# Two norms of a fused transformer block turned before their scale is known, with the scale spread as a row and multiplied in by VectorE

## The reference

```
y = x * rsqrt(mean(x * x) + 1e-6) * g              # layers
h2 = rms_norm(x, g_norm2) * (1 + sc2) + sh2        # first block, ahead of its feed-forward
u = rms_norm(h, mix_norm); proj = u @ w_in         # layers, ahead of the convolutions
dt, b, a = 48 small columns of proj                # gates of the two scans
```

## Time and profile before

| what | us |
|---|---|
| median of three runs (2225.5 to 2227.37) | 2226.86 |
| the profiled execution: its own time | 2223.37 |
| the profiled execution: its span | 2221.6 |
| PE busy | 2124.4 |
| DVE busy | 1329.9 |
| ACT busy | 1146.6 |
| POOL busy | 82.8 |

### The profile page before, as it was taken

The page is one execution under the profiler, slowest core; times in us unless marked ns, Lnnn a source line. Parts: engine busy times, 40 slices in busy tenths (PEclk is TensorE's granted clock), DMA queues, the critical chain, the costliest instruction groups (busy, mean ns, idle before and its releaser), DMA issues. The chain is left out here.

```text
span 2221.6 us, 40709 instructions
## 1 busy us (share of the span) xinstructions
PE 2124.4 (96%) x15572; PEld 1860.2 (84%) x15572; DVE 1329.9 (60%) x1821; ACT 1146.6 (52%) x1697; POOL 82.8 (4%) x90
## 2 busy tenths in 40 slices
PE   5999889999999999989999999999999998999998
PEld 4787778887888998888998887887998897998887
DVE  3436375556555996565656555555897565756554
ACT  3453644445445567654445445444557664535444
POOL 0000000000000010100000000000002010000000
PEclk9999999999999999999999999999999999999999
DMA  9663235554553544421455554555354431345553
GB/s 400 241 245 114 77 140 190 189 186 173 185 185 141 183 170 143 170 96 58 152 183 187 188 188 172 189 189 185 137 190 152 155 112 55 137 181 180 189 189 123
DMA packets 53325, 373.16 MB, mean 168 GB/s; under 512 B 6305, under 2 KB 6305, under 8 KB 9281
## 3 DMA queue, kind: packets, MB, share of 16 engines
q1 hardware_dynamic: 47664, 342.00, 42.0%
q0 software_dynamic: 5520, 29.23, 3.8%
HBM read 370.10 MB, written 1.11 MB: 167 GB/s over the span
## 5 line engine op out<-in xcount | busy, mean ns | idle before, releaser
L1470 ACT ACTIVATE HI<-ring 128x1024 fp32r<-128x1024 f32 x606 | 625.1, 1054 | 741.0 <-PE banks L549 399.2
L2020 DVE TENSOR_TENSOR LO<-ring,HI 128x1024 fp32r<-128x1024 f32 x318 | 389.1, 1226 | 369.8 <-ACT HI L1470 369.6
L2026 DVE TENSOR_TENSOR LO<-ring,HI 128x2048 fp32r<-128x2048 f32 x137 | 314.2, 2294 | 241.9 <-ACT HI L1470 241.9
L513 PE MATMUL banks<-UH,HI 128*128 128x256 f32 x1424 | 416.0, 292 | 2.7 <-DVE LO L2026 2.7
L514 PE MATMUL banks<-UL,HI 128*128 128x256 f32 x1424 | 404.0, 284 | 0.0
L515 PE MATMUL banks<-UH,LO 128*128 128x256 f32 x1424 | 403.7, 284 | 0.0
L547 PE MATMUL banks<-HI,UH 128*128 128x512 f32 x896 | 350.1, 391 | 7.1 <-DVE LO L2026 4.9
L548 PE MATMUL banks<-LO,UH 128*128 128x512 f32 x896 | 349.4, 390 | 0.0
L549 PE MATMUL banks<-HI,UL 128*128 128x512 f32 x896 | 349.2, 390 | 0.0
L513 PEld LDWEIGHTS banks<-UH,HI 128*128 128x128 f32 x1424 | 274.0, 192 | 20.5 <-issue 19.3
L514 PEld LDWEIGHTS banks<-UL,HI 128*128 128x128 f32 x1424 | 274.3, 193 | 1.9 <-issue 1.7
(11 more groups left out here) (329 smaller groups left out, 3058.1 us busy)
## 6 DMA issues: line engine op xcount, KB each, us to landing
ring<-in_w_stream SPq DMA_DIRECT2D x315, 1024.0 KB, 4.8
ARENA<-in_ada_stream POOLq DMA_DIRECT2D x16, 1024.0 KB, 5.1
ARENA<-in_ada_stream SPq DMA_DIRECT2D x8, 1024.0 KB, 15.1
GRMS<-cum_rows POOLq DMA_DIRECT2D x16, 256.0 KB, 3.6
ARENA<-in_na_bias POOLq DMA_DIRECT2D x2, 1024.0 KB, 15.2
RMS<-cum_rows POOLq DMA_DIRECT2D x8, 256.0 KB, 3.7
RSTD<-cum_rows POOLq DMA_DIRECT2D x8, 256.0 KB, 3.5
ARENA<-in_ropes POOLq DMA_DIRECT2D x1, 1088.0 KB, 20.7
```

Of the source, the lines that this page charges most:

```text
L513: nc.tensor.matmul(out, lh, rh, start=start, stop=False, **kw)
L1470: nc.scalar.activation(HI[:, q % PARTS, at], ring[:, q % RING, at], ACT.Copy).then_inc(hi_ready, 1)
L2020: nc.vector.tensor_tensor(LO[:, q % PARTS, at], ring[:, q % RING, at], HI[:, q % PARTS, at].bitcast(F32), ALU.subtract).then_inc(lo_ready, 1)
L2026: nc.vector.tensor_tensor(LO[:, q % PARTS, :], ring[:, q % RING, :], HI[:, q % PARTS, :].bitcast(F32), ALU.subtract).then_inc(lo_ready, 2)
```

## The change

Norms 1, 3 and 6 no longer build diagonals. PE transposes H unscaled (`raw_turns`) as soon as its pieces are in. When the reciprocal root is there, PE spreads it into PSUM bank 3 with two float32 products (a column broadcast against the identity), so that each partition holds the 256 tokens' scales in a row. DVE copies this row to SBUF, and makes U with one instruction a tile: turned rows times gain times scale row. In norm 1 the shift no longer goes into U: ACT adds it while it writes UH, tile by tile, and DVE while it writes UL. In the layers the small products are spread over panel 0: two tiles of k of them stand ahead of the products of each pair. The loop over panels 0 to 11 is written out, and panel 6 takes the plain order of products.

```diff
             def scaled_turns(d, banks):
-                pe.wait_ge(diag_ready, d + 1)
+                pe.wait_ge(scale_ready, d + 1)
...
+            def spread_scale(n):
+                pe.wait_ge(nrstd_ready, n + 1)
+                for t in range(2):
+                    mm = spread_tokens(bank[3][:, t * P:(t + 1) * P], NRSTD[:, t:t + 1])
+                mm.then_inc(scale_ready, 1)
+
+            def raw_turns(n, banks):
+                for p in range(KT // 2):
+                    turn_rows(n, p, banks[p])
+                spread_scale(n)
...
-            def both_tiles(outs, src, fill):
+            def both_tiles(outs, src, fill, beside=None):
...
+                    if beside is not None:
+                        beside(pair)
                     pe.wait_ge(uh_ready, KT * fill + 2 * pair + 2)
...
-            scaled_turns(1, TURN_BANKS)
+            raw_turns(1, TURN_BANKS)
...
-                scaled_turns(2 + l, TURN_BANKS)
+                raw_turns(3 + 3 * l, TURN_BANKS)
                 pe.wait_ge(pack2_loaded, 16 * l + 16)
-                for k in range(KT):
-                    pe.wait_ge(u_ready, KT * (2 + l) + k + 1)
-                    for t in range(2):
-                        mm = nc.tensor.matmul(bank[7][:, t * SMALL:(t + 1) * SMALL], ...)
-                mm.then_inc(small_done, 1)
-                with pe.Fori(0, (L_CONV - SCAN_CONV) // ROUND - 1) as r:
-                    for s in range(ROUND):
-                        wide(w0 + r * ROUND + s, ..., fill + 1 if s == 0 else None)
+                def small_products(pair):
+                    for k in (2 * pair, 2 * pair + 1):
+                        pe.wait_ge(u_ready, KT * (2 + l) + k + 1)
+                        for t in range(2):
+                            mm = nc.tensor.matmul(bank[7][:, t * SMALL:(t + 1) * SMALL], ...)
+                    if pair == KT // 2 - 1:
+                        mm.then_inc(small_done, 1)
...
+                conv_panel(0, fill + 1, small_products)
+                for j in range(1, L_CONV - SCAN_CONV - ROUND):
+                    conv_panel(j)
...
-                fill_high(u_ready, lambda k: KT * d + 2 * k + 2)
+                if shift is None:
+                    fill_high(u_ready, lambda k: KT * d + 2 * k + 2)
+                    return
+                for k in range(KT):
+                    act.wait_ge(u_ready, KT * d + k + 1)
+                    nc.scalar.activation(UH[:, k, :], U[:, k, :], ACT.Identity, bias=shift[:, k:k + 1]).then_inc(uh_ready, 1)
...
+            def raw_fill(n, d, fill, gain, shift=None, banks=TURN_BANKS):
+                dve.wait_ge(scale_ready, d + 1)
+                need(step(nc.vector.tensor_copy(RSTD[:, 0:S], bank[3][:, 0:S])))
+                def low(p):
+                    if shift is None:
+                        fill_low(fill, p)
+                        return
+                    for k in (2 * p, 2 * p + 1):
+                        dve.wait_ge(uh_ready, KT * fill + k + 1)
+                        nc.vector.scalar_tensor_tensor(UL[:, k, :], U[:, k, :], shift[:, k:k + 1], UH[:, k, :].bitcast(F32),
+                                                       ALU.add, ALU.subtract).then_inc(ul_ready, 1)
+                for p in range(KT // 2):
+                    dve.wait_ge(turned_done, 4 * n + p + 1)
+                    for e in range(2):
+                        k = 2 * p + e
+                        nc.vector.scalar_tensor_tensor(U[:, k, :], bank[banks[p]][:, e * S:(e + 1) * S], gain[:, k:k + 1],
+                                                       RSTD[:, 0:S], ALU.mult, ALU.mult).then_inc(u_ready, 1)
+                    if p:
+                        low(p - 1)
+                low(KT // 2 - 1)
...
-            diagonals(1)
-            scaled_fill(1, FILL_B1_NORM2, GS[:, 8:16], shift2)
+            raw_fill(1, 1, FILL_B1_NORM2, GS[:, 8:16], shift2)
...
-                diagonals(3 + 3 * l)
-                scaled_fill(3 + 3 * l, fill + 1, pk2("mix", 0, 8))
+                raw_fill(3 + 3 * l, 2 + l, fill + 1, pk2("mix", 0, 8))
```

More of the change, by code:

```diff
@@ L303, in build_program @@
             sem("residual_ready"), sem("squares_ready"), sem("sumsq_ready"))
-        rms_ready, nrstd_ready, diag_ready, turned_done, u_ready = (
-            sem("rms_ready"), sem("nrstd_ready"), sem("diag_ready"), sem("turned_done"), sem("u_ready"))
+        rms_ready, nrstd_ready, scale_ready, turned_done, u_ready = (
+            sem("rms_ready"), sem("nrstd_ready"), sem("scale_ready"), sem("turned_done"), sem("u_ready"))
         wide_free = sem("wide_free")
@@ L572, in both_tiles, with wide @@
                 return mm
-            def wide(w, q, rounds, par, fill=None):
+            def wide(w, q, rounds, par, fill=None, beside=None):
                 if fill is not None:
@@ L578, in wide @@
                     pe.wait_ge(wide_free, w + 1)
-                    both_tiles((bank[4 + par],), src, fill).then_inc(panel_used, 2)
+                    both_tiles((bank[4 + par],), src, fill, beside).then_inc(panel_used, 2)
                     return
@@ L987, in _, with conv_panel @@
                 ffn(1 + 2 * l, Q_LAYERS + LQ_FFN1, rounds, fill, turns(2 + 3 * l, TURN_BANKS))
-                scaled_turns(2 + l, TURN_BANKS)
+                raw_turns(3 + 3 * l, TURN_BANKS)
                 pe.wait_ge(pack2_loaded, 16 * l + 16)
-                for k in range(KT):
-                    pe.wait_ge(u_ready, KT * (2 + l) + k + 1)
-                    for t in range(2):
-                        mm = nc.tensor.matmul(bank[7][:, t * SMALL:(t + 1) * SMALL], U[:, k, t * P:(t + 1) * P],
-                                              pk2("small_w", k * SMALL, SMALL), start=(k + t == 0), stop=(k == KT - 1),
-                                              skip_group_check=True)
-                mm.then_inc(small_done, 1)
-                with pe.Fori(0, (L_CONV - SCAN_CONV) // ROUND - 1) as r:
-                    for s in range(ROUND):
[L1002 to L1006, removed]
+                def small_products(pair):
+                    for k in (2 * pair, 2 * pair + 1):
+                        pe.wait_ge(u_ready, KT * (2 + l) + k + 1)
+                        for t in range(2):
+                            mm = nc.tensor.matmul(bank[7][:, t * SMALL:(t + 1) * SMALL], U[:, k, t * P:(t + 1) * P],
+                                                  pk2("small_w", k * SMALL, SMALL), start=(k + t == 0), stop=(k == KT - 1),
+                                                  skip_group_check=True)
+                    if pair == KT // 2 - 1:
+                        mm.then_inc(small_done, 1)
+                def conv_panel(j, fill=None, beside=None):
+                    wide(w0 + j, Q_LAYERS + LQ_WIDE + j, rounds, j % 2, fill, beside)
+                conv_panel(0, fill + 1, small_products)
+                for j in range(1, L_CONV - SCAN_CONV - ROUND):
+                    conv_panel(j)
                 def running_sums():
@@ L1522, in norm_rows, with norm_whole @@
                 root(n)
-            def norm_whole(n, d, after=None, squared=0):
+            def norm_whole(n, d, after=None, squared=0, shift=None):
                 for j in range(squared, 4):
@@ L1694, in _ @@
             split(Q_WO + 2 + PARTS)
-            norm_whole(1, 1, after=(Q_FFN0 + 1,), squared=2)
+            norm_whole(1, 1, after=(Q_FFN0 + 1,), squared=2, shift=MOD[:, 24:32])
             ffn(0, Q_FFN0, 0, (ONES[:, 0:1], ONES[:, 0:1]))
@@ L2048, in diagonals @@
                     ins = nc.vector.tensor_scalar(DIAG[:, t, :], con("ident"), NRSTD[:, t:t + 1], None, ALU.mult)
-                ins.then_inc(diag_ready, 1)
+                ins.then_inc(scale_ready, 1)
             def turned_low(n, p, fill, gain, banks):
```

## The result

The changed kernel takes 2234.49 us (median of 11 runs, 2231.82 to 2237.46), the kernel before on the same chip 2225.96 (2221.95 to 2228.94). The ratio is 1.0039, 95% interval 1.0031 to 1.0046: 8.5 us slower, where 5.8 were forecast. The profiled execution took 2234.68 us against 2223.37, 11.3 more, at a span of 2232.9 and a mean granted clock of 0.982 (before 0.986).

A forecast was written before the change was run, and what follows sets the result against it. PE, busy 96% of the span, was taken as the bound. Norm 1 at +1.2 us and two layers at 2.3 each made +5.8 on the median 2226.86, so 2232.7 us, range 2220 to 2238.

The forecast's parts named there:

- The path up to UL: Layers' norms: transposes hidden in idle time, then spread, copy and U; first U pair some 0.7 us sooner than today.
- rival D: U itself is held by POOL: the forecast plus 3 us, 2236; chance 0.06.
- C: Rival: UL gets past POOL, 2.1 us saved a layer, 2219.3 in all; chance 0.12.
- The pause: Layers' norms: PE waits 3.1 us for the first UL, held to POOL's end; 3.8 us in norm 1.
- The fall of the clock: Behind the new pause PE drops to half speed for one 3.4 us stretch, costing 1.7 us a layer.
- the predicted full-clock times: Layers' norms without a clock fall: gates 13.2 us behind the reciprocal, panel 2 at 21.8.
- The wait for LO at panel 2: Layers' norms: late gates delay LO, PE waits 1.5 us at panel 2, each layer loses 0.55 us at full clock.
- the upper bound of +10.2: Whole kernel with two low stretches everywhere: norm 1 at 2.3 plus layers at 7.9 us.
- Norm 1: Pause of 3.8 us; 1.1 us sooner at full clock, +0.6 with one low stretch, +2.3 with two; taken as +1.2.
- The cover in the kernel before: Layers' norms before: UL held by POOL costs PE nothing, since PE is still turning or making small products.
- The written-out loop: Loop over panels 0 to 11: priced at nothing, since PE is full in the already written-out first panels too.
- Rival B: The pauses come but the clock hardly falls: 0.0 us change, 2226.9; chance 0.22.

The follow-up runs named there:

- e2: Changed kernel with LO of panel 1 in the layers' norms written by DVE instead of POOL: 2220.45 us, ratio 0.9976 to the kernel before.
- f1: Changed kernel, POOL's subtraction kept, PE given idle products in its waits in the layers' norms: 2223.15 us, ratio 0.9992 to the kernel before.
- e4: Kernel before with LO of panel 1 in the layers' norms written by DVE instead of POOL: 2221.05 us, ratio 0.9979 to the kernel before.
- e5: Only norm 1 as in the changed kernel, the layers' norms as in the kernel before: 2226.38 us, ratio 1.0009 to the kernel before.
- u1: Kernel before with only its loop over panels 0 to 11 written out: 2223.49 us, ratio 0.9990 to the kernel before.
- e3: Changed kernel with small products in one block ahead of panel 0 and the layers' LO of panel 1 by DVE: 2224.27 us, ratio 0.9993.
- f4: Changed kernel with small products in one block, the layers' LO of panel 1 by DVE, and 3 + 8 idle PE products: 2224.81 us, ratio 0.9995.
- f5: Changed kernel, small products in one block, LO of panel 1 by DVE in layers and norm 1, idle PE products in both: 2213.87 us, ratio 0.9945.
- e1: Changed kernel with the layers' small products in one block ahead of panel 0, POOL's subtraction kept: 2229.99 us, ratio 1.0024 to the kernel before.
- f2: Changed kernel with the layers' LO of panel 1 by DVE and 3 + 8 idle PE products around the spread: 2219.93 us, ratio 0.9972.
- f3: Kernel before with the layers' LO of panel 1 by DVE and 22 idle products in PE's wait for the diagonals: 2220.87 us, ratio 0.9980.
- f6: Changed kernel with small products in one block, POOL's subtraction kept, idle PE products in short gaps and the wait for U: 2223.06 us, ratio 0.9990.

## Why the prediction was right, and where it was off

**The path up to UL: right.** Transposes over 0.3 us before the reciprocal; spread 0.71 us for 0.6, copy 0.42, U 0.42 each (1.66 for four) for 0.45. UL was issued 3.06 us behind the reciprocal (predicted 2.93) and ended 6.94 behind it (6.92), 0.55 behind POOL. The four U straddle POOL's start at 705.78 and none was held, so rival D is out; UL came 1.2 us behind POOL's start, so C is out.

**The pause: right.** 2.78 us for 3.1; 3.13 in norm 1. e2 shows that it is POOL's: the same instruction took 0.69 us once POOL had nothing to do.

**The fall of the clock: right in kind, wrong in size.** This is the mis-sized term. I put one stretch of 3.4 us at half speed into each layer, 1.7 us. From the end of the pause to the end of panel 1 there are 0.48 + 7.08 + 5.76 = 13.3 us of work at full clock; it took 20.0 in norm 3 (710.92 to 730.9) and 16.1 in norm 6 (1569.8 to 1585.9), so the low clock cost 6.7 and 2.8 us. I had read the length of a low stretch off two norms in which PE was turning (3.4 us in norm 3, 6.8 in norm 1), took the shorter, and carried it over to a panel with small products mixed in. What makes the stretch long there isn't shown. That the clock is the term f1 proves: with the clock held, gates and panel 2 fall on the predicted full-clock times within 0.1 us.

**The wait for LO at panel 2: right in norm 6 (1.32 us for 1.5), absent in norm 3.** The low clock delays two chains, the small products with gates, split and LO behind them, and PE's panels. Against the predicted full-clock times the gates came 5.1 and 2.7 us late (18.37 and 15.91 for 13.2), the panels 6.7 and 2.8. The later chain sets panel 2, and PE had the 1.5 us of its wait in hand: 0.55 + 5.2 = 5.7 in norm 3, where the wait is used up, and 0.55 + 2.6 = 3.1 in norm 6, where 1.32 of it is left. The form of the sum held; its low-clock term was 1.7 instead of 5.2 and 2.6. Norm 3 alone lay above the 3.95 us that I had set as the most a layer could lose. The two layers were priced at 4.6 us and cost 8.8 in the profiled execution. The three norms together cost 9.3, close to the upper bound of +10.2, and the total lay inside the range only because the range reached that far.

**Norm 1: about right.** The clock was low for 6.8 us (322.93 to 329.76), and 3.0 of them lay in the pause itself, where they cost nothing; the rest cost what one stretch was priced at. The two profiled executions differ by +0.5, all traces together by about +1.0. I had worked out +0.6 for one stretch and +2.3 for two and took +1.2 between them, with no row for the choice.

**The cover in the kernel before: wrong.** "Today this costs PE nothing" held for the profiled norms and not for all executions (e4, and norm 6 of e5 and u1). The change did not create the lock's price; it exposed more of it.

**The written-out loop: priced at nothing, right within what can be told.** Rival B (clock hardly falls) gave 2226.9; f1, where it doesn't fall, came to 2223.2, so its mechanism is confirmed with 3.7 us of it on the good side unexplained.

## What to carry to other kernels

A wait that the bottleneck engine meets early, with little work ahead of it, is to be priced twice: the pause, and the work behind it at the lower clock, for as long as rows with the same kind of work show and not as rows with other work do. One execution is little to read that from: the same code kept the clock in one norm and lost it in the next (e2), and had a longer wait in one execution than in another (norm 6 of before, e5, u1). Before moving work to make a path shorter, look for what holds the next instruction on it (here POOL's subtraction on DVE's UL), and take that away first, by itself: here that alone (e4) gained as much as it did together with the change (e2), within what the intervals can tell. A cover that rests on a slow stretch is no cover in the executions in which that stretch runs fast.

## What the runs showed of the hardware

- PE's records can be full while the granted clock stays at 0.50: e2's norm 6 (12.00 of 12.00 us busy, 13.7 us low), and 14.8 us behind the pause in the changed kernel's norm 3. A low stretch lasted 3.4 us in the turns of norms 3 and 6 before, 6.8 in norm 1 before and in the changed kernel, 6.8 with the block of small products in e3, f4 and f5, 10.2 in e1, 10.2 and 17.1 with them mixed in. In norm 6 of e5 and u1 it was 3.4, at the end of the block and the start of panel 0. What sets its length no run isolates.
- It also fell without a long pause: in f4 among the 16 small products, with waits of 0.17 and 0.32 us.
- Products that compute nothing held it at 1.00 in both layers' norms of f1, f2, f3 and f6, and did not in f4 and f5. The Trainium skill ("TensorE: Matmul & The Clock Gate", Part 1) has the clock given up in idle PE time and released again by activity; the pauses here and f1 agree, while e2's norm 6 and f4 are low with full records, which that rule, read by the records, would not have.
- A DVE instruction of two SBUF tensors was held for as long as POOL's subtraction ran (3.88 us for 0.68; in norm 1 4.23 for a pair that takes 0.87 later), one of PSUM and an SBUF row beside it was not (0.42). The Trainium skill ("SBUF — State Buffer", the section on its two separate sides) has a VectorE instruction with two SBUF inputs shut out while a GpSimd instruction that reads SBUF and began first is running. These rows agree, and no run here has the other order.
